# A two-layer decoder step on one core: the SSD group's small steps placed between the matmuls of the input projection, and the SSD half of the output projection taken first

## The chip, the cores and the metric

The kernel runs on one core of a Trainium2 chip. The metric is the device time of one execution in microseconds (us). The core has a matrix engine (PE, whose weight loads are listed apart as PEld), a vector engine (DVE), a scalar engine (ACT), GpSimd (POOL) and a queue engine (SP) that here only starts DMAs. Each engine works through its own list of instructions in order and waits on semaphores where another engine's result is needed.

## The reference, cut to what matters

320 tokens (256 of a prompt and 8 sequences of 8) of width 1024 go through two layers. Each layer is a mixer and a feed-forward part; layer 0 has a dense one, layer 1 a mixture of 8 experts.

```python
def parallel_mixer(hn, lb, w_in, conv_w, ..., w_out, s_hg, s_ssd, conv_buf):
    proj = jnp.einsum('bld,de->ble', hn, w_in)
    q, f, i, og, z, xbc, dt = jnp.split(proj, SPLIT_IDX, axis=-1)
    q = silu(q); log_f = logaddexp(log(lb), log1p(-lb) + log_sigmoid(f)); k_in = (1 - lb) * sigmoid(-f)
    o_hg, s_hg_new = hgrn2_chunked(q, k_in, i, log_f, s_hg)
    o_hg = rmsnorm(o_hg, hg_norm) * silu(og)
    conv = silu(conv_b + sum(conv_w[tap] * xpad[:, tap:tap + L]))   # 4 taps over xbc
    xs, bm, cm = jnp.split(conv, ...)
    dtf = softplus(dt + dt_bias); A = -exp(a_log)
    y, s_ssd_new = ssd_chunked(xs * dtf, dtf * A, bm, cm, s_ssd)
    y = rmsnorm((y + d_skip * xs) * silu(z), ssd_norm)
    return einsum('ble,ed->bld', concatenate([o_hg, y]), w_out), s_hg_new, s_ssd_new, conv_buf_new

for l in range(2):
    h = h + parallel_mixer(rmsnorm(h, norm_mix[l]), ...)
    h = h + (swiglu if l == 0 else moe_swiglu)(rmsnorm(h, norm_ffn[l]), ...)
return rmsnorm(h, norm_final), states
```

## The kernel before, in words

All matrix products with weights are done in three passes: a weight is split into a rounded high part (`spH`, made by ACT in `split_hi`) and the rest (`spL`, made by DVE in `split_lo`), and the activations likewise (`hnH`, `hnL`). PE runs high x high, high x low and low x high. Weights arrive in units of 1 MB in a ring of six places that SP fills; `split_hi` and `split_lo` turn a unit into one of two split buffers, and PE raises `used` when it has read one. A unit of the input projection is 32 matmuls with `spH` and 16 with `spL`, 320 columns each.

One layer's mixer has three stages on PE:

1. **The input projection**, 14 units: seven chunks of 512 output columns, each in two halves over the contraction, on PSUM banks 0 to 3 and 4 to 7 in turn. The order of the chunks is xs, B and C (together `xbc`), q, og, z, f, i. ACT evacuates each chunk. DVE runs the convolution over the first two chunks (`conv_in`), ACT its activation.
2. **The HGRN heads**: three token tiles (the 64 sample tokens first, then 128 and 128 prompt tokens; numbers 2, 0, 1) by four heads. For each head PE makes exponents (L1883, L1884), ACT their exponential (`M`), DVE the products (`Yq`, `Yk`), PE the scores (L1901 to L1908), DVE the mask (`SC`), PE the output (L1923). The states of the eight sample sequences lie in 16 slabs in the ring: eight of the HGRN group (k = 0), eight of the SSD group (k = 1). PE asks them (`ask`, L1960) in two steps for each group, ACT copies the answer (`said`), PE turns it (`turn_said`, L1968) and DVE adds it. Each HGRN slab is updated by a matmul (`sample_state`), an ACT scaling and a DVE add (`add_state`, L1375).
3. **The SSD group and the output projection.** After the last head PE goes through the SSD steps, for three tiles: transposes (`turn_tokens`, L1999, L2002), sums of the step sizes (`step_sums`, L2027), C times B (`groups`, L2051), decays from the start (`entry_sums`, L2039), the product inside a tile (`inside`, L2062), the prompt state (`prompt_ssd`, L2073), the carried state's part (L2154), and for the samples `ask(1, .)` and `sample_ssd` (L2089), whose slab is scaled by POOL and added to by DVE (`add_ssd`, L1352). Between them lie the squares for the HGRN norm (`group_squares`, L2100). Then come the four units of the output projection (`projected`, 7 us each): the HGRN half of the contraction on both column halves, the squares of the SSD group (L2212), and the SSD half.

The order within an engine is written out by hand in the source; there is no planner. SP loads the slabs after the output projection's weights, four slabs to a ring place, each place when the unit in it has been split.

Of the kernel before, what the change touches and what calls it, by code (L numbers as in the profile page):

```python
# [122 lines left out]
CHUNKS = [2560, 3072, 0, 1536, 2048, 512, 1024]  # L123
C_XS, C_BC, C_Q, C_OG, C_Z, C_F, C_I = range(7)
# [8 lines left out]
HG_BANKS = (2, 3, 2, 3)  # L133
# [7 lines left out]
ASK_AT = {(0, 1): 0, (0, 3): 1}  # L141
TOLD_AT = {(0, 2): 0, (1, 0): 1}
# [29 lines left out]
def build(nc, a, outs, table, at):  # L172
    y_prompt, y_sample, hg_p, ssm_p, conv_p, hg_s, ssm_s, conv_s = outs
    ctx = ExitStack()
    with ctx:
# [35 lines left out]
        def tabv(name, dt=F32):  # L211
            o, n = at[name]
            if o < nr:
# [21 lines left out]
        xdt = put("xdt", [P, NH * HD])  # L235
        xw = put("xw", [P, NH * HD])
        Bt = put("Bt", [P, G * P])
        SH = put("SH", [P, H * P])
        rstd = put("rstd", [P, TOK], offset=cursor[0] - 4 * H * P)
        SS = put("SS", [P, NH * HD])  # L240
        qGp = put("qGp", [P, H, P], offset=cursor[0] - 4 * NH * HD)
# [14 lines left out]
        wsm = put("wsm", [P, NH])  # L256
# [4 lines left out]
        cso = put("cso", [3 + NSQ * 3, CONV], offset=tok0 + 8 * CONV)  # L261
        Bm = put("Bm", [NS, NSQ, G * P], offset=tok0 + 17 * 1024)
# [8 lines left out]
        ea = put("ea", [P, NSQ * NH], offset=hn0 + 15 * 1024 + 512)  # L271
        am = put("am", [P, NSQ, NH], offset=hn0 + 15 * 1024 + 768)
        kd2 = put("kd2", [NS, H * P], offset=hn0 + 16 * 1024)
        vtk2 = put("vtk2", [NS, H * P], offset=hn0 + 18 * 1024)
        La = put("La", [P, NH, P], offset=ov + 4 * 1024)
        t1 = put("t1", [P, 4, P], offset=ov + 8 * 1024)
        CBm = put("CBm", [P, G, P], offset=ov + 10 * 1024)
        Mt = {2: M, 0: put("M2", [P, LV + 1, P], offset=tok0 + 4 * 1024), 1: M}
        Lat = {2: put("La2", [NS, NH, NS], offset=tok0), 0: La, 1: put("La1", [P, NH, P], offset=arena + 8 * H * TOK)}
        aext = {2: put("aex2", [NS, NH, HD], offset=tok0 + 2 * 1024)}  # L280
        xdtt = {2: xdt, 0: put("xdt1", [P, NH * HD], offset=tok0 + 2 * 1024), 1: xdt}
        xwt = {2: put("xw2", [NS, NH * HD], offset=hn0 + 16 * 1024), 0: xw,
               1: put("xw1", [P, NH * HD], offset=tok0)}
        Btt = {2: put("Bt2", [NS, G * P], offset=hn0 + 18 * 1024), 0: Bt, 1: Bt}
        EE2 = put("EE2", [P, 4, NS], offset=hn0 + 19 * 1024)
        aex = put("aex", [P, NH, HD], offset=sc0)
        aext[1] = aex
# [9 lines left out]
        sqs = put("sqs", [P, 4, TOK], offset=arena + 4 * H * TOK)  # L297
        rsh = put("rsh", [P, H, TOK], offset=arena + 8 * H * TOK)
# [90 lines left out]
        def slab(l, k):  # L389


            return ring[:, (PLAN["out", l] + 4 + k // 4) % RING, 512 * (k % 4):512 * (k % 4) + 512]
# [1303 lines left out]
        def _(pe):  # L1696
# [78 lines left out]
            for l in range(DEPTH):  # L1775
# [96 lines left out]
                def exponents(t, h):  # L1872
# [3 lines left out]
                    if j:  # L1876

                        pe.wait_ge(S("x_exp"), j)
# [561 lines left out]
```

## Time and profile before

| | us |
|---|---|
| median of 3 runs | 1767.23 (1765.89 to 1770.63) |
| the profiled execution | 1772.5, its span 1770.7 |
| mean granted clock of PE, share of full | 0.975 |
| PE busy | 1705.9 (96%) |
| DVE busy | 1291.2 (73%) |
| ACT busy | 1039.1 (59%) |
| POOL busy | 98.3 (6%) |

A row of the timeline gives start, duration, engine, line, operation, output and inputs, and in brackets how long the engine had been idle before it and what ended that. A row of the table by stretch gives, for each engine, the busy time and the number of instructions, then PE's granted clock (1.00 is 2.4 GHz, 0.50 is 1.2 GHz) and what the DMA engines moved. The profiled execution took 1.8 us more than its span. The stages after the mixers (dense feed-forward of layer 0, experts of layer 1) take from 272.7 to 525 us and from 775 us to the end.

### The profile page before, as it was taken

To read this page: it belongs to the slowest core of one execution; us is meant where nothing else is said; L and a number is where in the kernel's file an instruction comes from. 1 tells how busy PE (TensorE), PEld (TensorE's weight loads), DVE (VectorE), ACT (ScalarE), POOL (GpSimd) and SP (SyncE) were. 2 spreads that over 40 slices of the span, in tenths; PEclk is the share of its full clock that TensorE was granted. 3 is DMA by queue.
4 is the path that set the end of the run, shared out by engine and by line. 5 is a ranking of instruction groups with operands and counts; after the bars stand their busy time and mean duration, and the time that the engine had idled before them with its cause. 6 is when DMAs were issued, how large, how long until landed. Compare 5 with 4: busy or idle time off the path is not lost.

```text
span 1770.7 us, 23227 instructions
## 1 busy us (share of the span) xinstructions
PE 1705.9 (96%) x9594; PEld 1484.9 (84%) x9594; DVE 1291.2 (73%) x1119; ACT 1039.1 (59%) x942; POOL 98.3 (6%) x85
## 2 busy tenths in 40 slices
PE   8999889999999999789999999999999999999997
PEld 7988778999999978678888888888888888788876
DVE  6636655444357347649988888888888888888897
ACT  4444333333334344247777777777777777777776
POOL 2001120000000011202200000000000000000200
PEclk9997989999999989899999999999999999999999
DMA  9559153443553413249999999999999999899994
GB/s 298 167 162 269 49 171 115 155 148 99 147 169 121 165 39 84 60 179 331 391 394 396 397 371 384 374 382 395 362 379 379 368 397 389 317 394 370 373 394 175
DMA packets 272616, 474.07 MB, mean 268 GB/s; under 512 B 41578, under 2 KB 103266, under 8 KB 272504
## 3 DMA queue, kind: packets, MB, share of 16 engines
q1 hardware_dynamic: 266432, 452.37, 71.7%
q10 hardware_dynamic: 3368, 12.75, 2.2%
q0 software_dynamic: 2704, 7.39, 1.5%
q8 instruction: 78, 1.28, 0.3%
q14 instruction: 34, 0.28, 0.0%
HBM read 454.69 MB, written 29.84 MB: 274 GB/s over the span
## 4 chain that ended last, share of the span: by engine, by line
PE 88%; DVE 6%; issue 2%; ACT 2%; DMA 1%; ACTq 0%; DVEq 0%
PE ps L1712 16%; PE ps L1713 16%; PE ps L2355 11%; PE ps L1707 9%; PE ps L1708 9%; PE ps L2376 5%; PE ps L1806 4%; PE ps L2241 3%; PE ps L1923 2%; DVE spL L1592 1%; PE ps L2259 1%; PE ps L2394 1%; PE ps L1901 1%; PE ps L2203 1%; DMA ring<-in_w_exp_in_dram 1%
## 5 line engine op out<-in xcount | busy, mean ns | idle before, releaser
L1592 DVE TENSOR_TENSOR spL<-ring,spH 128x2048 fp32r<-128x2048 f32 x336 | 767.2, 2292 | 100.2 <-ACT spH L967 97.6
L967 ACT ACTIVATE spH<-ring 128x2048 fp32r<-128x2048 f32 x336 | 643.0, 1916 | 131.9 <-PE ps L2355 69.0
L1712 PE MATMUL ps<-spH,XH 128*128 128x512 f32 x896 | 354.6, 396 | 1.8 <-issue 1.8
L1713 PE MATMUL ps<-spH,XL 128*128 128x512 f32 x896 | 350.4, 391 | 0.0
L1050 DVE TENSOR_TENSOR spL<-ring,spH 128x2048 fp32r<-128x2048 f32 (+1 forms) x74 | 158.8, 2146 | 182.3 <-ACT spH L662 182.2
L1707 PE MATMUL ps<-hnH,spH 128*128 128x320 f32 x928 | 277.3, 313 | 4.0 <-DVE hnL L1065 2.2
L1708 PE MATMUL ps<-hnL,spH 128*128 128x320 f32 x928 | 275.6, 311 | 0.0
L662 ACT ACTIVATE spH<-ring 128x2048 fp32r<-128x2048 f32 (+1 forms) x74 | 133.5, 1804 | 187.7 <-PE ps L2241 73.6
L2355 PE MATMUL ps<-spL,XH 128*128 128x512 f32 x896 | 240.9, 391 | 1.2 <-DVE spL L1592 1.2
L2355 PEld LDWEIGHTS ps<-spL,XH 128*128 128x128 f32 x896 | 168.0, 188 | 38.3 <-DVE spL L1592 2.4
L1712 PEld LDWEIGHTS ps<-spH,XH 128*128 128x128 f32 x896 | 168.7, 188 | 36.1 <-issue 2.3
L1713 PEld LDWEIGHTS ps<-spH,XL 128*128 128x128 f32 x896 | 168.9, 189 | 34.0
L1707 PEld LDWEIGHTS ps<-hnH,spH 128*128 128x128 f32 x928 | 176.4, 190 | 7.4 <-issue 4.8
L1708 PEld LDWEIGHTS ps<-hnL,spH 128*128 128x128 f32 x928 | 176.4, 190 | 0.2
L1712 PE MATMUL ps<-spH,hTH 128*128 128x512 f32 x448 | 175.9, 393 | 0.0
L1713 PE MATMUL ps<-spH,hTL 128*128 128x512 f32 x448 | 175.0, 391 | 0.0
L2376 PE MATMUL ps<-spL,hTH 128*128 128x512 f32 x444 | 119.3, 390 | 0.0
L1712 PEld LDWEIGHTS ps<-spH,hTH 128*128 128x128 f32 x448 | 84.1, 188 | 17.8 <-issue 0.2
L1713 PEld LDWEIGHTS ps<-spH,hTL 128*128 128x128 f32 x448 | 84.2, 188 | 17.4
L2376 PEld LDWEIGHTS ps<-spL,hTH 128*128 128x128 f32 x444 | 83.3, 188 | 18.3 <-DVE spL L1592 0.5
L1806 PE MATMUL ps<-hnH,spL 128*128 128x320 f32 x448 | 70.3, 309 | 0.0
L991 ACT ACTIVATE hTH<-ps 128x512 fp32r<-128x512 f32 x56 | 33.6, 600 | 60.7 <-PE ps L2394 60.7
(365 smaller groups left out, 1796.2 us busy)
## 6 DMA issues: line engine op xcount, KB each, us to landing
ring<-in_w_exp_in_dram SPq DMA_DIRECT2D x224, 1024.0 KB, 8.8
ring<-in_w_exp_out_dram SPq DMA_DIRECT2D x112, 1024.0 KB, 8.7
ring<-in_w_in_dram SPq DMA_DIRECT2D x28, 1024.0 KB, 5.4
ring<-in_w_ffn_in_dram SPq DMA_DIRECT2D x22, 1024.0 KB, 5.1
token_rows<-token_rows ACTq DMA_DIRECT2D x1, 11776.0 KB, 40.5
ring<-in_w_ffn_out_dram SPq DMA_DIRECT2D x16, 704.0 KB, 4.6
ring<-in_w_out_dram SPq DMA_DIRECT2D x8, 1024.0 KB, 5.0
out_dram<-ring SPq DMA_DIRECT2D x32, 256.0 KB, 2.7
```

Source lines behind the costliest of these rows:

```text
L662: A(spH[:, u % 2, 0:n], raw(u, n), ACT.Copy).then_inc(S("hi_done"), 1)
L967: A(esplit(j)[0], src, ACT.Copy).then_inc(S("hi_done"), 1)
L1050: V.tensor_tensor(spL[:, u % 2, 0:n], raw(u, n), spH[:, u % 2, 0:n].bitcast(F32), ALU.subtract).then_inc(S("split_done"), 1)
L1592: V.tensor_tensor(lo, eslot(j)[0], hi.bitcast(F32), ALU.subtract).then_inc(S("split_done"), 1)
L1707: mm(out, w, x[0], start=start, stop=False)
L1708: return mm(out, w, x[1], start=False, stop=False)
L1712: mm(out, x[0], w, start=start, stop=False)
L1713: return mm(out, x[1], w, start=False, stop=False)
L1806: m = mm(ps[:, 4 * (c % 2) + i, 0:TOK], wL[:, k, i * P:(i + 1) * P], hnH[:, kk], start=False, stop=kk == KT - 1)
L2241: m = mm(ps[:, 4 * (j % 2) + 2 * half + i, 0:TOK], wL[:, k, i * P:(i + 1) * P], hnH[:, k], start=False, stop=k == KT - 1)
L2355: m = mm(ps[:, 2 * (c % 2) + i // 2, :], XH[:, kk, xs], wL[:, k], start=False, stop=kk == KT - 1)
L2376: m = mm(ps[:, 6 + q, :], tH[:, f], wL[:, k, 512 * q:512 * q + 512], start=False, stop=c == EC - 1 and f == 3)
```

## The change: what it does

Everything concerns the two mixers; the line numbers of the changed kernel differ.

- The chunks of the input projection come in the order xs, BC, f, i, q, z, og. The first two are as before. The other five are cut into ten units of 256 output columns by the whole contraction, `whole(0)` to `whole(9)`, on banks 0, 1 and 2, 3 in turn. Banks 4 to 7 are free for SSD steps.
- A unit has three slots for other PE work: after the high passes of its first 128 columns, after those of its second, and after its low passes. All SSD steps over tiles stand there, and so does the turning of the convolution state (`turn_conv`, before: right after the projection). Their DVE and ACT parts stand between the splits. ACT loads its function tables four times in a mixer where it did twice.
- In the HGRN heads the SSD slabs are asked first, at (2, 1) and (2, 3) (tile, head), the HGRN slabs at (0, 1) and (0, 3) as before. The product with z, the squares of the SSD group and its norm are done during the heads; one unit of the output projection is split at (2, 1), the other already in the input projection (before: at (0, 0) and (0, 1)). POOL scales all eight SSD slabs in one row after `ask(1)`. SP loads the SSD slabs first.
- The output projection takes the SSD half first. `sample_ssd(1)`, `group_squares(0)`, `sample_ssd(2)` and `group_squares(1)` stand between the column groups of its first unit, `sample_ssd(3)` behind it, `sample_ssd(0)` before the last head's output.

```diff
-CHUNKS = [2560, 3072, 0, 1536, 2048, 512, 1024]
-C_XS, C_BC, C_Q, C_OG, C_Z, C_F, C_I = range(7)
+CHUNKS = [2560, 3072, 512, 1024, 0, 2048, 1536]
+C_XS, C_BC, C_F, C_I, C_Q, C_Z, C_OG = range(7)
+NARROW = 10
...
-ASK_AT = {(0, 1): 0, (0, 3): 1}
-TOLD_AT = {(0, 2): 0, (1, 0): 1}
+ASKS = ((1, 0), (1, 1), (0, 0), (0, 1))
+ASK_AT = {(2, 1): 0, (2, 3): 1, (0, 1): 2, (0, 3): 3}
+TOLD_AT = {(2, 2): 0, (0, 0): 1, (0, 2): 2, (1, 0): 3}
...
+                def whole(k, slots):
+                    u, h = PLAN["in", l] + 4 + k, k % 2
+                    if k < 2:
+                        pe.wait_ge(S("proj_evac"), NARROW * l + 1)
+                    elif k < 4:
+                        pe.wait_ge(S("f_evac"), 2 * l + h + 1)
+                    else:
+                        pe.wait_ge(S("proj_evac"), NARROW * l + k - 1)
+                    pe.wait_ge(S("hi_done"), u + 1)
+                    wH, wL = unit(u, KT)
+                    for i in range(2):
+                        for kk in range(KT):
+                            high(ps[:, 2 * h + i, 0:TOK], wH[:, kk, i * P:(i + 1) * P], (hnH[:, kk], hnL[:, kk]),
+                                 start=kk == 0)
+                        for step in slots[i]:
+                            step()
+                    pe.wait_ge(S("split_done"), u + 1)
...
+                    for step in slots[2]:
+                        step()
...
+                whole(0, ((), (), ()))
+                whole(1, ((), (), ()))
+                whole(2, ((turn_conv,), (lambda: step_sums(2),), (small_sums, lambda: turn_inputs(2))))
+                whole(3, ((lambda: step_sums(0),), (lambda: turn_groups(2),), (lambda: step_sums(1),)))
+                whole(4, ((lambda: groups(2),), (lambda: entry_sums(2, 1, 4), lambda: entry_sums(1, 2, 5)),
+                          (lambda: inside(2),)))
+                whole(5, ((lambda: turn_inputs(0),), (lambda: turn_groups(0),), (lambda: groups(0),)))
+                whole(6, ((lambda: prompt_ssd(0, 5),), (lambda: inside(0),), (lambda: turn_inputs(1),)))
+                whole(7, ((lambda: turn_groups(1),), (lambda: groups(1),), (from_carried,)))
+                whole(8, ((lambda: inside(1),), (lambda: prompt_ssd(1, 4),), ()))
+                whole(9, ((), (), ()))
...
+                def forget_part(h):
+                    dve.wait_ge(S("used"), u + 4 + h + 1)
+                    V.tensor_scalar(lfT[:, 2 * h:2 * h + 2], ps[:, 2 * h:2 * h + 2, 0:TOK], -40.0, None, ALU.max
+                                    ).then_inc(S("f_evac"), 1)
...
                 def sample_ssd(j):
                     pe.wait_ge(S("mask_done"), 8 * l + 4 + j + 1)
-                    if j == 0:
-                        pe.wait_ge(S("xw_done"), LT(l, 2) + 1)
-                        pe.wait_ge(S("E_exp"), 2 * l + 1)
+                    if j == 1:
                         pe.wait_ge(S("sh_done"), 2 * l + 2)
-                    if j == 1:
-                        pe.wait_ge(S("ss_done"), 2 * l + 1)
                     pe.wait_ge(S("slab_done"), 16 * l + 8 + 2 * j)
...
                     scores(t, h)
                     if j + 1 == len(HEADS):
-                        turn_tokens(2)
+                        sample_ssd(0)
+                    if (t, h) in ((1, 1), (1, 2)):
+                        ssd_squares(h - 1)
...
-                step_sums(2)
-                groups(2)
-                entry_sums(2, 1, 4)
-                turn_tokens(0)
-                ask(1, 0)
...
-                projected(0)
-                pe.wait_ge(S("gsq_done"), 2 * l + 2)
...
+                projected(0, (lambda: sample_ssd(1), lambda: group_squares(0), lambda: sample_ssd(2),
+                              lambda: group_squares(1)))
+                sample_ssd(3)
                 projected(1)
```

In `projected`, `half, c = divmod(i, 2)` becomes `half, c = 1 - i // 2, i % 2`, and unit 1 waits for `slab_done` of all 16 slabs and for the second `grs_done`.

The first place is DVE in layer 0's input projection, right after the convolution; `cpk` is the packed convolution state, `spL` the low part of a unit, `lfT` the forget gates. Before:

```order
L1143 SCALAR_TENSOR_TENSOR cvt<-xbc,vec,cvt 128x344 x3
L1050 TENSOR_TENSOR spL<-ring,spH 128x2048
L1209 COPY cpk<-xbc 128x8x3
L1211 COPY cpk<-xbc 128x24 x8
L1050 TENSOR_TENSOR spL<-ring,spH 128x2048 x7
L1179 TENSOR_SCALAR lfT<-ps 128x1280
L1184 SCALAR_TENSOR_TENSOR kT<-kT,lbom,lfT 128x320 x4
```

And the same place in the changed kernel:

```order
L1164 SCALAR_TENSOR_TENSOR cvt<-xbc,vec,cvt 128x344 x3
L1071 TENSOR_TENSOR spL<-ring,spH 128x2048
L1200 COPY cpk<-xbc 128x8x3
L1202 COPY cpk<-xbc 128x24 x8
L1209 TENSOR_SCALAR lfT<-ps 128x640
L1294 SCALAR_TENSOR_TENSOR dtb<-dtb 128x24
L1296 SCALAR_TENSOR_TENSOR dtb<-dtb,bc 128x24
L1300 TENSOR_TENSOR am<-dtb,tab 64x64
L1219 TENSOR_TENSOR La_111<-tabR,dtb 64x512
L1209 TENSOR_SCALAR lfT<-ps 128x640
L1071 TENSOR_TENSOR spL<-ring,spH 128x2048
```

The evacuation of the forget gates, last of all before, now comes right behind the convolution, in two parts, and PE's third narrow unit waits for the first of them.

The second place is DVE between the last heads and the output projection; `ring` is a slab, `rss` and `rsh` the norms' factors of the SSD and the HGRN half, `hnL` the projection's input. Before, its last steps of the mixer:

```order
L1437 TENSOR_TENSOR cvT<-cvT,zT 128x1280
L1441 SCALAR_TENSOR_TENSOR oT<-oT,vec,rsh 128x320 x4
L1352 TENSOR_TENSOR ring<-ring,ps 128x512 x2
L1446 TENSOR_TENSOR hnL<-oT,hnH 128x1280
L1352 TENSOR_TENSOR ring<-ring,ps 128x512 x2
L1452 SCALAR_TENSOR_TENSOR cvT<-cvT,vec,rss 128x320 x4
L1456 TENSOR_TENSOR hnL<-cvT,hnH 128x1280
```

In the changed kernel, from the last HGRN slab (L1442) on; L1433 is the prompt's HGRN state:

```order
L1442 TENSOR_TENSOR ring<-ring,ps 128x512 x2
L1473 SCALAR_TENSOR_TENSOR cvT<-cvT,vec,rss 128x320 x4
L1419 TENSOR_TENSOR ring<-ring,ps 128x512 x2
L1480 TENSOR_TENSOR hnL<-cvT,hnH 128x1280
L1433 SCALAR_TENSOR_TENSOR SH<-SH,egp,ps 128x128 x4
L1419 TENSOR_TENSOR ring<-ring,ps 128x512 x2
L1485 TENSOR_TENSOR oT<-oT,ogT 128x1280
L1419 TENSOR_TENSOR ring<-ring,ps 128x512 x2
L1489 SCALAR_TENSOR_TENSOR oT<-oT,vec,rsh 128x320 x4
L1419 TENSOR_TENSOR ring<-ring,ps 128x512 x2
L1494 TENSOR_TENSOR hnL<-oT,hnH 128x1280
```

The SSD half's input, the last of all before, now comes behind the first of four `add_ssd`; the last `add_ssd` stands behind the HGRN norm.

The third place is PE in the heads of the sample tile, before (exponents, output, scores, exponents of the next head):

```order
L1883 MATMUL ps<-tabR,lfH 128x256
L1884 MATMUL ps<-tabR,lfL 128x256
L1923 MATMUL ps<-SC,vtk_109 128x64 x4
L1901 MATMUL ps<-Yq_103,Yk_104 64x64 x3
L1904 MATMUL ps<-qT,kT 64x64
L1883 MATMUL ps<-tabR,lfH 128x256
L1884 MATMUL ps<-tabR,lfL 128x256
L1923 MATMUL ps<-SC_105,vtk_109 128x64 x4
```

and in the changed kernel:

```order
L2058 MATMUL ps<-tabR,lfH 128x256
L2059 MATMUL ps<-tabR,lfL 128x256
L2135 MATMUL ps<-ring,cvT 32x128 x16
L2100 MATMUL ps<-SC,vtk_105 128x64 x4
L2076 MATMUL ps<-Yq_101,Yk_102 64x64 x3
L2079 MATMUL ps<-qT,kT 64x64
L2058 MATMUL ps<-tabR,lfH 128x256
L2059 MATMUL ps<-tabR,lfL 128x256
L2143 MATMUL ps<-tab,said 128x128 x4
L2100 MATMUL ps<-SC_103,vtk_105 128x64 x4
```

One `ask` (16 matmuls) and one `turn_said` (4 transposes) have come in; the same pair stands at heads (2, 3) and (0, 0).

## Rows read from the trace of the kernel before

**Rows 1.** The table by stretch: the stages of both mixers.

```profile
16.27:120.18 103.91, 103.40 (x707) 101.41 (x707) 60.13 (x88) 48.46 (x67) 0.00 (x0) 1.00 0.62 204
120.18:201.51 81.33, 74.76 (x560) 62.87 (x559) 47.36 (x78) 33.20 (x66) 8.29 (x8) 0.81 0.66 197
201.51:272.67 71.16, 61.91 (x480) 55.40 (x479) 40.66 (x66) 22.79 (x31) 15.80 (x13) 0.90 0.46 132
...
629.12:704.86 75.74, 69.15 (x560) 58.08 (x559) 47.40 (x78) 32.95 (x66) 8.35 (x8) 0.89 0.23 53
704.86:775.20 70.34, 61.09 (x472) 53.04 (x471) 40.56 (x66) 19.73 (x29) 16.25 (x15) 0.93 0.31 87
```

**Rows 2.** PE's timeline in layer 0: its waits, and one ask at either clock.

```profile
54.47 2.51 PE L1806 MATMUL ps<-hnH,spL 128*128 128x320 f32 x16
...
121.76 1.03 PE L1833 MATMUL ps<-tab,cpk 128*27 128x128 f32 x8 [1.42 <-ACT oT L767]
...
125.02 0.38 PE L1883 MATMUL ps<-tabR,lfH 64*128 64x256 f32 x1 [1.79 <-DVE lfL L1220]
...
154.19 1.08 PE L1960 MATMUL ps<-ring,qG 128*32 128x128 f32 x32
...
186.17 1.56 PE L1984 MATMUL ps<-vtk,kdm 32*128 32x128 f32 x16 [1.11 <-DVE ring L1375]
...
193.52 1.60 PE L1923 MATMUL ps<-SC,vtk 128*128 128x128 f32 x12 [1.05 <-DVE SC L1260]
...
216.44 1.09 PE L2062 MATMUL ps<-M,xdt 128*64 128x128 f32 x16 [2.69 <-DVE M L1300]
217.46 1.94 PE L1960 MATMUL ps<-ring,cvT 128*32 128x128 f32 x32
...
238.03 2.08 PE L2089 MATMUL ps<-xw,Bm 32*128 32x256 f32 x8 [5.60 <-DVE ring L1352]
```

**Rows 3.** Groups by line of PE's work from 198.3 to 240 us, shapes apart.

```profile
L2027 PE MATMUL ps<-tabR,La 128*128 128x128 f32 x32 | 4.0, 278 | 0.0
...
L2100 PE MATMUL ps<-sqh,tab 128*128 128x320 f32 x8 | 2.6, 446 | 0.0
...
L2005 PE MATMUL ps<-dtb,tabR 64*64 64x8 f32 x2 | 0.3, 210 | 0.0
```

**Rows 4.** DVE's timeline, layer 0.

```profile
64.95 0.75 DVE L1211 COPY cpk<-xbc 128x24 f32<-128x24 f32 x8
...
110.51 1.48 DVE L1179 TENSOR_SCALAR lfT<-ps 128x1280 f32<-128x1280 f32 x1
...
199.33 1.28 DVE L1375 TENSOR_TENSOR ring<-ring,ps 128x512 f32<-128x512 f32 x2
...
232.30 1.61 DVE L1437 TENSOR_TENSOR cvT<-cvT,zT 128x1280 f32<-128x1280 f32 x1
234.75 1.94 DVE L1441 SCALAR_TENSOR_TENSOR oT<-oT,vec,rsh 128x320 f32<-128x320 f32 x4 [0.84 <-ACT rsh L909]
```

**Rows 5.** ACT's timeline, layer 0: the HGRN norm.

```profile
232.47 0.94 ACT L905 ACTIVATE rsh<-ps,eps 128x320 f32<-128x320 f32 x2 [3.48 <-PE ps L2100]
233.45 1.27 ACT L909 ACTIVATE rsh<-rsh 128x1280 f32<-128x1280 f32 x1
```

**Rows 6.** The table by stretch, finer: around changes of the granted clock.

```profile
121.91:125.32 3.41, 1.62 (x14) 1.33 (x13) 0.68 (x1) 1.66 (x3) 1.02 (x2) 1.00 0.29 94
125.32:128.73 3.41, 3.41 (x16) 2.08 (x15) 1.08 (x5) 1.95 (x4) 0.00 (x0) 0.50 1.03 357
...
149.21:152.63 3.42, 3.42 (x20) 3.07 (x18) 0.00 (x0) 2.50 (x3) 0.00 (x0) 0.50 0.97 315
...
214.07:217.48 3.41, 1.04 (x19) 0.90 (x20) 3.38 (x7) 0.00 (x0) 1.07 (x1) 1.00 0.00 0
217.48:220.89 3.41, 3.41 (x38) 2.67 (x37) 3.38 (x7) 0.00 (x0) 0.00 (x0) 0.50 0.71 158
...
630.53:633.94 3.41, 1.69 (x13) 1.43 (x14) 0.68 (x1) 1.57 (x4) 1.02 (x2) 1.00 0.03 7
...
654.42:657.84 3.42, 3.42 (x20) 3.02 (x20) 0.21 (x1) 2.38 (x2) 0.00 (x0) 0.50 0.00 0
```

More of the change, by code:

```diff
@@ new lines, in _ @@
+                tables(LN_EXP)
+                act.wait_ge(S("gate_steps"), 4 * l + 2)
+                own(A(dtb[:, 2], dtb[:, 1], ACT.Exp, scale=-1.0))
+                A(dtb[:, 2], dtb[:, 2], ACT.Ln, bias=1.0).then_inc(S("dt_ln"), 1)
+                if l == 0:
+                    act.wait_ge(S("stage_in"), 16)
+                    A(tabR[:], stage[:], ACT.Copy).then_inc(S("setup_act"), 1)
+                split_hi(u + 7)
+                act.wait_ge(S("f_evac"), 2 * l + 2)
+                own(A(kT[:], lfT[:], ACT.Exp, scale=-1.0))
@@ new lines, in _ @@
+                act.wait_ge(S("gate_steps"), 4 * l + 4)
+                act.wait_ge(S("setup_dve"), 3)
+                for h in range(H):
+                    A(lfT[:, h], lfT[:, h], ACT.Ln, bias=lbom[:, l, 0, h:h + 1],
+                      scale=lbom[:, l, 1, h:h + 1]).then_inc(S("lf_done"), 1)
+                evacuated(2)
+                split_hi(u + 8)
+                act.wait_ge(S("w_mm"), l + 1)
+                for i, t in enumerate(ORDER):
+                    n = TILES[t][1]
+                    A(wsm[0:n, i], ps[0:n, 7, 256 + 8 * i:264 + 8 * i], ACT.Exp)
@@ new lines, in turn_conv, with sums @@
+                def turn_conv():
+                    pe.wait_ge(S("cpk_done"), 8 * (l + 1))
+                    pe.wait_ge(S("proj_evac"), NARROW * l + 2)
+                    for half in range(2):
+                        for k in range(4):
+                            m = nc.tensor.transpose(ps[0:27, 6 + half, k * P:(k + 1) * P], cpk[:, 4 * half + k, :], ident)
+                        m.then_inc(S("cso_tr"), 1)
+                def sums(t):
+                    return tabv("w")[:, LV * P:] if t < 2 else tabv("ws")[0:NS, LS * NS:]
@@ L1816, in _, with from_carried @@
+                def from_carried():
+                    pe.wait_ge(S("ss_done"), 2 * l + 1)
+                    for j in range(4):
+                        m = mm(ps[:, 5, j * P:(j + 1) * P], SS[:, j * P:(j + 1) * P], cvT[:, 6 + j // 2, P:2 * P],
+                               start=True, stop=True)
+                    m.then_inc(S("yx_mm"), 1)
+                for c in (C_XS, C_BC):
+                    if c == C_XS and l:
                         pe.wait_ge(S("rstd_done"), 2 * l + 1)
-                    if c == 1:
+                    if c == C_BC:
```

912 lines of the change are left out of this document (449 added, 463 removed).

## The prediction

> **What bounds the kernel now.** I read the table by stretch first, then PE's timeline. PE is busy 103.40 of the 103.91 us of layer 0's input projection: there PE itself is the bound, while DVE works 60.13 and ACT 48.46 us [rows 1]. In the heads and in the last stage PE has 6.6 and 9.3 us without work, and a granted clock of 0.81 and 0.90 [rows 1]. The waits of the last stage are few and long: 2.69 us for the masked decays `M`, 5.60 us for the second last slab addition behind the HGRN norm; in the heads 1.42 and 1.79 us at the entry and 1.11 and 1.05 us near the end [rows 2]. So an SSD step that is laid into the projection costs its own PE time there; only the waits and the half clock that follows them can be won.
>
> What they are worth: layer 0's waits after the projection are 15.9 us (81.33 + 71.16 less 74.76 + 61.91, with the rounding), and the clock of 0.90 over 71.16 us is some 10 to 14 us at half clock, of which 5.6 were idle; that is about 4 us. An ideal change would win about 20 us in a layer. The question is what it puts in their place.
>
> **The change part by part,** layer 0; the time of a unit of weights is 7.04 us (48 passes; the last 16 of them show as 2.51 us with their drain, 2.35 from start to start [rows 2]).
>
> a) *Input projection, work.* From 198.3 to 240 us the SSD steps that move there make 17 of the 26 groups, L2027's with 4.0 us the largest and L2005's with 0.3 the smallest [rows 3]; together 20.9 us, with `turn_conv` (1.03 us [rows 2]) 21.9. About 1 us of it is half clock. Every group's busy time ends later than the next one starts, by about 0.1 us, 22 to 25 times. I take 18.3 us. Bounds: 16.5 and 21.9.
>
> b) *Input projection, waits.* PE's third narrow unit waits for the evacuation of the first. DVE reaches it only behind the convolution and the packing, 65.7 us [rows 4], and it takes half of 1.48 us with its fixed part, 0.8. PE has finished two narrow units at 63.9 (49.8 and twice 7.04). The wait is 66.6 less 63.9, 2.7 us. I followed the remaining units by the rows' durations: DVE's split of a unit comes when ACT's is done, and ACT's when the unit two before has been read. Everything a slot needs is there, but for the mask of tile 0, which stands behind a split: 0.3 us. Sum 3.0. The other end is 9, 1 us at each of six units; its lower end is 2.4, as the first wait can't go.
>
> c) *Entry to the heads.* Before: 120.18 to 125.02, 4.8 us with `turn_conv` in it [rows 1, 2]. After: ACT evacuates half a chunk and loads a table, then the same chain of two copies; 3.6 us. Gain 1.2.
>
> d) *Asks among the sample tile's heads.* Twice an `ask` and a turning. The stretch runs at 1.2 GHz today: 27.3 us in layer 0 (eight rows from 125.32 to 152.63) and 17.1 in layer 1 (five rows, the last ends at 657.84) [rows 6]. There an ask costs 1.94 us instead of 1.08 [rows 2] and the turning about 1.0: 5.9 us. At full clock it is 3.4 and a wait of 1.1 behind the split at head (2, 1), which is then in DVE's way: 4.5. I take 5.9.
>
> e) *Later in the heads.* The product with z, 1.61 us [rows 4], stands ahead of the low gates that PE's next exponents wait for; about 0.6 us of it is covered: +1.0 (0 to 1.6). The SSD squares are four fp32 matmuls of 320 columns, like L2100's (2.6 us for four [rows 3]); they fall just ahead of the waits of 1.11 and 1.05 us [rows 2] and fill them: +0.2 (0 to 2.6).
>
> f) *The last head.* `sample_ssd(0)` needs the PSUM banks of the last HGRN slab, whose additions end at 200.6 [rows 4]. PE stands 2.2 us, works 1.1, then makes the last output, which before could start behind 1.3 us of transposes: +2.0.
>
> g) *From the last output to the end of the output projection,* before 71.16 us [rows 1]. After: the prompt state 1.0, a wait of 0.4 for `add_ssd(0)` and of 0.6 for `hnL`; four units 28.2; three `sample_ssd` 3.4 (2.08 in the row is at half clock [rows 2]); the two `group_squares` 2.6 less drains, 2.5. Then a new wait: unit 1 needs all slabs, and the last addition stands on DVE behind the norm. From the second squares ACT needs 0.94 and 1.27 [rows 5], DVE 1.94 and 1.3 [rows 4]: 5.6 with the hand-overs, of which 3.5 are covered by the low passes and `sample_ssd(3)`: 2.2. Sum 38.3. Gain 32.9 in layer 0, 32.0 in layer 1.
>
> Sum of a to g: 18.3 + 3.0 - 1.2 + 5.9 + 1.0 + 0.2 + 2.0 - 32.9 = -3.7 us in layer 0, -2.8 in layer 1.
>
> h) *POOL beside the heads.* Its eight scalings of slabs (part of 15.80 us busy [rows 1]) move to the first heads of the prompt tile. The trace has no such overlap there. Nothing if DVE never meets it, 3.6 if two of DVE's products each wait one scaling of up to 1.8. I take 1.0 a layer.
>
> i) *Half clock after the new waits.* A stretch with PE busy 1.04 of 3.41 us was followed by one at 0.50 [rows 6], which costs half of its 3.4 us where PE has work. There are three new candidates a layer (2.7 us in b; 2.2, 0.4 and 0.6 close together in f and g; 2.2 in g). Taken as an even chance each and rounded down: +1.7. Bounds 0 and 5.1.
>
> Total: -3.7 - 2.8 + 2.0 + 3.4 = -1.1; the half clock in the heads that followed the wait of 1.11 us in layer 0 may go with that wait, -1.7. That makes -2.8 us. The profiled execution took 1772.5 us, so 1769.7 in its terms; the runs' median is 1767.2, so 1764.5.
>
> *Hidden otherwise:* ACT's two extra table loads lie in the projection, where ACT works under half the time. The SSD slabs come when units 12 and 13 of the projection have been split, some 15 us before the first ask; SP's weight loads for the next stage start about 17 us before they are needed (24 before). The 11.8 MB of zeros that ACT starts in layer 0 still start at the entry to the heads.
>
> **A rule against the change.** Both layers enter the heads with PE busy 1.62 and 1.69 us of a stretch of 3.41, much of it transposes (L1833 and the gates'). In layer 0 the clock fell at once, in layer 1 it stayed at 1.00 two stretches longer [rows 6]. The Trainium skill says in "TensorE: Matmul & The Clock Gate", Part 4: PE-mode transpose, that transposes do not count as activity for the clock as matmuls do. By that rule both entries should have fallen; the trace agrees for one.
>
> **The rivals.**
> 1. *Both entries fall.* After the change only the gates' transposes stand in an entry of 3.6 us, so less work than in either row. Layer 1 then has the heads of layer 0: 81.33 less 75.74 is 5.6 us [rows 1], less 1.7 for a later stretch at half clock in layer 0: +3.9, so 1768.4. For it: less PE work; against it: the entry is shorter. The rule above would make this certain.
> 2. *The new waits and the half clock stay away* (faster). No half clock in i (-3.4), POOL meets nobody (-2.0), d at 4.5 (-2.8), e at nothing (-2.0): -10.2, so 1754.3; with half of these 1759. For it: PE's work in the slots fills the stretches; against it: each piece needs its own luck.
> 3. *DVE is late in the projection* (slower). Its chain is ACT's split, DVE's split, then an SSD step that the next slot reads; about 21 us of SSD work join the 60.13 [rows 1]. Should each of six units from the fourth to the ninth wait 1 us, that is +12 over both layers: 1776.5. It decides from about 0.7 us a unit. Against it: by the durations each step is ready 0.5 us or more before its slot, but for one.
> 4. *The steps don't land in the slots.* The order of PE shows them there; I give it nothing of weight.
>
> **How the numbers follow.** My forecast 0.35, rival 1 0.13, rival 2 0.31, rival 3 0.20, rival 4 0.01. The forecast's own range is 1760 to 1770. What a measurement can tell from no change is 0.3%, 5.3 us: faster is below 1761.9, slower above 1772.5. The forecast lies a tenth below 1761.9 and the rest between; rival 2 is faster, rival 3 mostly slower, and of rival 1 a quarter. Faster 0.35, same 0.42, slower 0.23. Likeliest 1764.5; the range takes in most of both sides: 1752 to 1777.
>
> **What would show it.** In the profile after: a wait of 2 to 3 us of PE for DVE's `lfT` in the projection of each layer, and that stage 21 us longer; waits of about 2 us ahead of `sample_ssd(0)` and of the output projection's second unit; 38 us from the last output to the projection's end; the heads 4 to 9 us longer. It is wrong if the projection grows by 27 or more (rival 3), if the clock stays at 1.00 through the entries, or if the last stage is not near 38.

## The result, and the profile after

The changed kernel took 1784.11 us (median of 5 runs, 1781.81 to 1787.9), the kernel before 1767.23 (5 runs, 1762.51 to 1774.47): a ratio of 1.0088, 95% interval 1.0066 to 1.011 (the ratio is taken over all runs of both; the quotient of the two medians is 1.0096). The forecast was 1764.5 us with a range of 1752 to 1777; the time lies above both. The profiled execution after has a span of 1780.0 us, against 1770.7.

The table by stretch of the kernel after (us, busy time of PE, PEld, DVE, ACT, POOL, granted clock, DMA share, GB/s) answers to [rows 1]: projection, heads and last stage of layer 0, then of layer 1; the last row leaves off the end of its stage.

```profile
15.41:142.90 127.49, 123.84 (x883) 119.13 (x884) 80.25 (x128) 58.32 (x91) 1.41 (x3) 0.99 0.56 170
142.90:241.32 98.42, 78.28 (x629) 64.96 (x627) 53.01 (x84) 35.66 (x67) 26.02 (x17) 0.80 0.53 170
241.32:279.71 38.39, 36.25 (x233) 33.61 (x232) 17.28 (x20) 13.10 (x12) 0.86 (x1) 0.97 0.71 205
532.28:658.22 125.94, 122.23 (x884) 117.65 (x885) 76.48 (x116) 54.76 (x86) 1.45 (x3) 1.00 0.39 113
658.22:742.00 83.78, 76.67 (x633) 63.87 (x631) 53.40 (x85) 36.24 (x68) 26.00 (x17) 0.86 0.20 56
742.00:778.70 36.70, 34.20 (x214) 31.42 (x214) 16.64 (x20) 9.43 (x9) 1.30 (x3) 0.95 0.41 116
```

What stands out is the second row: layer 0's heads take 98.42 us and layer 1's 83.78 for the same work; before they took 81.33 and 75.74 [rows 1]. PE has 20.1 us without work there. Its timeline in layer 0 says where, and answers to [rows 2]:

```profile
65.64 0.41 PE L1745 MATMUL ps<-hnH,spH 128*128 128x320 f32 x1 [2.47 <-DVE lfT L1209]
...
146.58 0.39 PE L2058 MATMUL ps<-tabR,lfH 64*128 64x256 f32 x1 [3.08 <-DVE lfL L1345]
...
189.51 0.87 PE L2135 MATMUL ps<-ring,qG 128*32 128x128 f32 x12 [13.65 <-DMA ring<-in_state_hgrn_dram]
...
236.43 1.17 PE L2171 MATMUL ps<-xw,kdm 32*128 32x256 f32 x5 [2.33 <-DVE ring L1442]
...
258.52 0.39 PE L1745 MATMUL ps<-hnH,spH 128*128 128x320 f32 x1 [2.14 <-issue]
```

Three of these five waits were in the forecast as waits, and the one of 3.08 us lies inside its entry of 3.6 us. The third was not: 13.65 us before `ask(2)`, the first ask of the HGRN slabs, in layer 0 alone. Before, the same ask stood there without a wait (154.19 in [rows 2]). The change loads the slabs in the other order, so the queues have to be read. SP's of the kernel before (start, issuing time, number of transfers):

```profile
103.58 9.06 SPq L457 DMA_DIRECT2D ring<-in_state_hgrn_dram  x8
155.98 12.68 SPq L457 DMA_DIRECT2D ring<-in_state_ssm_dram  x8
```

SP's of the kernel after:

```profile
122.76 11.04 SPq L462 DMA_DIRECT2D ring<-in_state_ssm_dram  x8
140.92 27.70 SPq L462 DMA_DIRECT2D ring<-in_state_hgrn_dram  x8
```

And the transfers of the kernel after from 140 to 190 us (KB each, median us from issue to landing):

```profile
token_rows<-token_rows ACTq DMA_DIRECT2D x1, 11776.0 KB, 45.8
ring<-in_state_hgrn_dram SPq DMA_DIRECT2D x8, 256.0 KB, 9.9
out_dram<-SS POOLq DMA_DIRECT2D x1, 256.0 KB, 6.1
```

The same zeros in the kernel before, which started at 122.8 us:

```profile
token_rows<-token_rows ACTq DMA_DIRECT2D x1, 11776.0 KB, 40.5
```

ACT starts the 11.8 MB of zeros at 143.11 us, and they land 45.8 us later, at 188.9. Before, the eight HGRN loads were issued by 112.6, ahead of the zeros, and the SSD slabs, which came under the zeros, were asked only behind 200 us. After, the HGRN slabs come in two fours, as places of the ring come free. The first four are issued from 140.9 to 142.4, ahead of the zeros, and land within 5.8 us. The other four are issued from 159.0 to 160.5, under the zeros:

```profile
DMA to landing us min/median/max: 14.0/23.3/28.9
```

They land one after another, 14.0, 21.4, 25.3 and 28.9 us after their issue, the last at 189.4. The first HGRN ask needs all eight and could have begun at 175.9: TensorE waits until 189.5. Layer 1 has no zeros and no such wait.

The rest of the ledger, by the two profiles: layer 0's mixer (projection to the end of its output projection) takes 7.9 us more, layer 1's 1.3 us less; without the 13.65 us they would be 5.8 and 1.3 us shorter. The start is 0.9 us shorter and the stretch behind layer 1's mixer 3.5 longer; about 4 us of that is idle time of TensorE near the start of the last expert pair, for which the trace names no engine:

```profile
1523.90 0.49 PE L1750 MATMUL ps<-spH,XH 128*128 128x512 f32 x1 [1.95 <-issue]
1529.23 0.59 PE L1751 MATMUL ps<-spH,XL 128*128 128x512 f32 x1 [3.91 <-issue]
```

The kernel before has one such wait, of 1.84 us. That makes 9 us in the profiles; the medians lie 17 apart, which is taken up below.

### The profile page after: what moved, and what is told of

The parts are those of the page before. It is cut to its first block, busy times and chain, and to the rows that moved or that the text cites. A ratio compares the mean times of both kernels' runs of the same rounds, so it can differ in the third digit from the quotient of the medians.

```text
span 1780.0 us, 23257 instructions
## 1 busy us (share of the span) xinstructions
PE 1705.6 (96%) x9594; PEld 1484.3 (83%) x9594; DVE 1295.3 (73%) x1121; ACT 1044.5 (59%) x956; POOL 106.6 (6%) x85
## 4 chain that ended last, share of the span: by engine, by line
PE 89%; DVE 5%; DMA 2%; issue 2%; ACT 1%; SPq 0%; DVEq 0%; ACTq 0%
PE ps L1750 17%; PE ps L1751 17%; PE ps L2419 11%; PE ps L1745 9%; PE ps L1746 8%; PE ps L2440 6%; PE ps L2305 3%; PE ps L1872 2%; PE ps L2100 2%; DMA ring<-in_state_hgrn_dram 2%; PE ps L2323 1%; PE ps L2458 1%; PE ps L2076 1%; PE ps L2271 1%; PE ps L1844 1%
## 5 line engine op out<-in xcount | busy, mean ns | idle before, releaser
L1750 PE MATMUL ps<-spH,hTH 128*128 128x512 f32 x448 | 175.9, 393 | 0.0
L1750 PEld LDWEIGHTS ps<-spH,hTH 128*128 128x128 f32 x448 | 84.1, 188 | 17.7
L1751 PEld LDWEIGHTS ps<-spH,hTL 128*128 128x128 f32 x448 | 84.2, 188 | 17.5
L2440 PEld LDWEIGHTS ps<-spL,hTH 128*128 128x128 f32 x444 | 83.4, 188 | 17.9
L642 POOL DMA_INDIRECT took<-token_rows,ixi x6 | 10.5, 1756 | 814.0 <-SPq L528 812.5
## 6 DMA issues: line engine op xcount, KB each, us to landing
token_rows<-token_rows ACTq DMA_DIRECT2D x1, 11776.0 KB, 45.8
```

What stands on the lines that cost most here:

```text
L1750: mm(out, x[0], w, start=start, stop=False)
L1751: return mm(out, x[1], w, start=False, stop=False)
L2440: m = mm(ps[:, 6 + q, :], tH[:, f], wL[:, k, 512 * q:512 * q + 512], start=False, stop=c == EC - 1 and f == 3)
```

## The experiments

Eleven edited kernels ran, and the changed kernel a second time, 5 to 12 executions each. Every ratio is to executions of the kernel before that were taken beside them; their medians were 1769.68 us for e1, e1p, c1 and e2, 1768.09 for e0, e3, e4 and e5, and 1769.57 for c2, e6, e7 and e8. Where kernels of different groups are compared below, a difference of medians therefore holds to a few us only, and the one by the ratios stands beside it.

**The zeros.** Three kernels: the changed one with the zeros later (e1), with 20 of their 23 blocks at the old place (e1p), and the kernel before with them later (c1).

```
-                if l == 0:
+                    if l == 0 and (t, h) == (0, 1):     # behind told(ASK_AT[t, h])
                     act.wait_ge(S("xs_zero"), 16)
                     act.dma_start(rows[CAP:, :]...)
```

> The changed kernel with one DMA moved: the 11.8 MB of zeros that ScalarE starts at the entry to layer 0's heads are started behind the third ask (head 1 of tile 0), when all sixteen slabs have landed. Theory A (the HGRN slabs, whose loads the change puts behind the SSD slabs, land only when the zeros have landed; that is the loss): the wait of 13.65 us before the third ask in layer 0 falls under 1 us, the asks behind it run at full clock, layer 0's stretch from the heads to the output projection falls from 98.4 to about 84 us (layer 1 has 83.8), and the time from 1784.1 to about 1769.5 (1766 to 1773). Rival B (the loads are slow by themselves, because SyncE issues eight of them in a row between 140.9 and 168.6 us): the wait stays over 8 us and the time over 1777. Rival C (the zeros take the same time from the slab stores and the weight loads that come next): the wait goes but over 5 us of it come back before the feed-forward layer, 1775 or more.

> The changed kernel with the zeros split in two transfers: 20 of the 23 blocks (10.2 MB) still start at the entry to the heads, 3 blocks behind the third ask. Theory A: the slabs land when the first transfer has landed; 45.8 us x 20/23 = 39.8 us, 6.0 us sooner, so the wait before the third ask falls from 13.65 to about 7.7 us (6 to 9.5) and the time by about 6 us, to 1778 (1775 to 1781). Rival B (slow loads by themselves): the wait stays within 1 us of 13.65. Rival D (it is the start of the big transfer that delays the loads, not its length): also unchanged.

> Control: the kernel before with the same move of the zeros (behind the first HGRN ask of tile 0). Its HGRN slabs land before the zeros start and its SSD slabs are asked some 20 us after the zeros have landed, so theory A expects no change: 1767.2, within 0.3% (1762 to 1772.5). If it gains 5 us or more, the zeros cost the kernel before something too, and the gain of the first run would say less about the change.

| kernel | median us | ratio [95%] | wait before `ask(2)` |
|---|---|---|---|
| after | 1784.11 | 1.0088 [1.0066, 1.011] | 13.65 |
| e1p, 20 of 23 blocks | 1779.55 | 1.0058 [1.004, 1.0076] | 7.89 |
| e1, zeros later | 1768.81 | 0.9989 [0.9971, 1.0007] | 0.49 |
| c1, before, zeros later | 1768.78 | 0.9994 [0.9974, 1.0014] | none |

The row of e1p and that of e1 at that ask:

```profile
185.99 1.94 PE L2138 MATMUL ps<-ring,qG 128*32 128x128 f32 x32 [7.89 <-DMA ring<-in_state_hgrn_dram]
```

```profile
177.21 1.08 PE L2135 MATMUL ps<-ring,qG 128*32 128x128 f32 x32 [0.49 <-DVE t L1410]
```

Theory A stands in what it says of the cause: the wait goes with the zeros, its length follows theirs (7.7 us were worked out beforehand for 20 blocks, 7.89 came), and the kernel before, whose order never puts a needed slab under them, gains nothing. In e1 the same eight loads land in 3.7 us (median, 5.0 at most), so rival B falls; the slab stores now take 8.7 us each under the zeros, but nothing came back from that (rival C). All three times lie in their ranges. The profile of e1p is of its second fastest execution (1770.41 us, with a median of 1779.55): that one escaped half clock in layer 1, as shown below. This one collision accounts for the loss: without it the time falls by 15.3 us (17.5 by the ratios), and e1 lies within 0.3% of the kernel before. In the profiles layer 0's heads take 82.0 us in e1 and 98.42 in the changed kernel, 16.4 more: the wait, and half clock for the ask and the matmuls behind it (1.94 us for the ask instead of 1.08).

The Trainium skill says in "DMA: Bandwidth & Descriptors", Queues, rings and completion order, that a DMA engine takes turns between queues packet by packet. This trace agrees, if what the profile counts as packets are the packets meant. The profile counts them for each queue (packets, MB, share of the DMA engines' time); in the kernel after, from 166 to 182 us, while zeros (q10) and loads (q1) run side by side:

```profile
q10 hardware_dynamic: 1166, 4.77, 85.5%
q1 hardware_dynamic: 1189, 0.59, 14.4%
```

That is one packet for one packet, but those of the zeros hold 4 KB each and those of the loads 0.5 KB (4.77 MB and 0.59 MB), so the loads get a ninth of the bytes. At that rate 1 MB in four loads takes some 28 us (an estimate: 2048 packets at 1189 in 16 us). So theory A's wording, that the slabs land when the zeros have landed, is too strong: three of the four land earlier, and the last, at 189.4, would by this estimate have come at about that time had the zeros gone on. A shorter transfer helps all the same (e1p), since the loads speed up when the zeros run out: from 182 to 188 us q1 moves 719 packets.

**The first wait in the projection.** In e2 the instruction `forget_part(0)` stands ahead of the last `conv_in`.

> The changed kernel with one VectorE instruction moved: the first copy of the forget gate's products out of the banks (0.82 us) is issued before the last of the eight convolutions instead of behind the eighth, a split and the packing of the convolution state. Theory: TensorE's wait of 2.47 us before the third 256-column unit goes in both layers (to under 0.2), nothing else moves by over 0.5 us, and the time falls by 4.9 us to 1779.2 (1777 to 1782). Rival: the split of the next unit, now 0.8 us later, is then the last thing in that unit or the convolution is, and under 2 us are gained (1782 or more).

Measured: 1775.01 us, 1.0028 [1.0013, 1.0044], below the range; the wait of 2.47 us is gone in both layers, and nothing took its place. That is 9 us under the changed kernel (10.6 by the ratios) and not 4.9; layer 1's heads were 2.6 us shorter (79.7 for 82.3) at more clock, so part of the surplus is of the kind treated next. A term of the forecast that I had called unavoidable (its "lower end is 2.4, as the first wait can't go") went by moving one instruction.

**The changed kernel again.** A surplus as in e2, and 17 us between medians where the profiles give 9, asked for a second timing.

> The changed kernel, not edited, timed again beside the kernel before: the recorded ratio of 1.0088 rests on five runs of each. In the two profiled executions the mixers account for +6.6 us, the start for -0.9 and the stretch behind the second mixer for +3.5 (9.3 us together), but the medians lie 17 us apart. If the difference of the profiles is the true one, the ratio comes out near 1.005; if the medians' is, near 1.009. I expect 1.008 (1.0065 to 1.009), 1783 us: in the changed kernel's profile both entries to the heads fall to half clock, and in the one run of the zeros experiments in which layer 1's entry did not, its heads took 76 instead of 82 us; the kernel before may escape that more often than its one profile shows.

Measured: 1783.67 us, 1.0083 [1.007, 1.0096]. The difference of the medians is real.

**The clock behind the entry.** Of the changed kernels, e1p had one layer whose heads took 76 us instead of 82. The stretch of 20 us that begins 4 us behind the entry's start, in layer 1 of e1 (the clock is the third number from the end):

```profile
650.20:670.20 20.00, 20.00 (x126) 15.41 (x128) 9.44 (x24) 6.25 (x10) 8.64 (x4) 0.52 0.20 56
```

The same of e1p:

```profile
658.40:678.40 20.00, 17.80 (x170) 13.65 (x169) 14.17 (x29) 8.62 (x13) 13.12 (x7) 0.91 0.19 55
```

At 0.52 (1.2 GHz for nearly all of it) PE is busy without a gap and makes 126 matmuls; at 0.91 (mostly 2.4 GHz) it makes 170 and has time left. Ahead of both stands the idle wait of 3.07 us at the entry, so the wait alone doesn't fix how long the clock stays down. In e5 it is filled, in c2 a part of the one of the kernel before.

```
                 turn_gates(ORDER[0])
+                hold(12, 5)          # e5, on e1: 12 unread matmuls of 512 columns
+                hold(6, 1)           # c2, on the kernel before
                 exponents(ORDER[0], 0)
```

> The kernel of e1 (zeros behind the third ask) with 12 matmuls of 128x512 whose result nobody reads, put on TensorE behind the gates' transposes at the entry to the heads of each layer, into a free bank: some 2.7 us of work in a wait of 3.07 us. Nothing else is moved and nothing can be saved but clock. Theory E (the wait at the entry is what drops the clock to 0.50 for some 20 us behind it): the clock stays at 1.00 from the entry on, the heads of each layer take 76 instead of 82 us as in the one execution in which layer 1's entry stayed up, and the time falls from 1768.8 to 1757 (1754 to 1761). Rival F (the clock falls for what the sample tile's heads themselves are, small matmuls with gaps): it falls all the same, and the time stays at 1768.8 (1766 to 1771).

> Control for e5: the kernel before with 6 matmuls of 128x512 (some 1.4 us) in its wait of 1.79 us at the entry to the heads, nothing else. If what the held entry gives back (17.7 us from e1 to e5, of which 5 lie behind the second mixer) is a property of both kernels, the kernel before gains too: its profile shows half clock from 4 to 32 us behind layer 0's entry and from 12 to 28 behind layer 1's. But it has two more idle pieces at the entry (1.42 us before the turning of the convolution's state) that stay. Theory E: 1760 (1756 to 1766). If it stays at 1768 (1766 to 1771), the held entry is worth something in the changed kernel alone, and the change made the entry worse for the clock.

e5: 1751.12 us, 0.9903 [0.989, 0.9916]; c2: 1764.39, 0.9976 [0.9958, 0.9995]. The same stretch in layer 0 and 1 of e5:

```profile
149.10:169.10 20.00, 18.30 (x174) 14.17 (x173) 14.47 (x29) 8.87 (x14) 12.41 (x7) 0.91 0.19 55
644.20:664.20 20.00, 18.37 (x175) 14.22 (x174) 14.42 (x29) 8.96 (x14) 12.65 (x7) 0.91 0.20 58
```

Matmuls that compute nothing save 17.7 us by the medians, 15 by the ratios, more than the range had: rival F falls, and theory E stands for the entry, where the clock is 1.00 for the first 12 us. It isn't 1.00 throughout: 16 us behind the entry a stretch of 4 us has 0.66 in layer 0, hence the 0.91. The heads take 77.7 us in both layers instead of 82.0 and 82.8, though the unread matmuls stand in them; that is 9.4 of the 17.9 us between the profiles of e1 and e5. Another 5.3 lie behind layer 1's mixer, where e5 lacks the second of the two unexplained waits, and 3.0 in the two last stages; why, no run here tells. The kernel before gains 5.2 us from the same trick (4.2 by the ratios), within the range of its forecast: its entry costs it something too, but less. So the changed kernel had both entries at half clock in the profiles of itself (0.53 and 0.53), of `e0_after_again` (0.53 and 0.51) and of e1 (0.54 and 0.52), while the kernel before had 0.50 and 0.63 (c2: 0.74 and 0.63). How much of the 8 us between profiles and medians this is stays open: that kernel's runs spread over 12 us (1762 to 1774), and its profiled run (1772.5) lies in their upper part.

**Real work in the same wait.** e4 puts `ask(0)` there and ACT's table load behind its copy of the gates; e6 adds the four masked copies of POOL behind the second ask.

```
                 turn_gates(ORDER[0])
+                ask(0)
-ASK_AT = {(2, 1): 0, (2, 3): 1, (0, 1): 2, (0, 3): 3}
+ASK_AT = {(2, 2): 1, (0, 1): 2, (0, 3): 3}
+                pool.wait_ge(S("ask_mm"), 4 * l + 2)      # e6, ahead of the masked copies
```

> The kernel of e1 with real work in the entry's wait: the first ask of the SSD slabs goes from head 1 of the sample tile to right behind the gates' transposes (1.08 us at full clock), the second from head 3 to head 2, and ScalarE copies the turned gates before it loads its table (1.28 us) and not after. The wait of 3.07 us should shrink to 3.07 - 1.28 - 1.08 = 0.7 us, and the stretch lose 1.28 + 1.94 (an ask at half clock) = 3.2 us a layer whatever the clock does: 1768.8 - 6.4 = 1762.4. If theory E holds and 0.7 us of idle time is little enough, 6 us a layer come on top: 1750. I expect 1751 (1748 to 1764).

> The kernel of e4 with GpSimd's four masked copies of the keys (2.1 us each) behind the second ask, out of the sample tile's heads. In e4 VectorE's short steps beside them took 1.20, 1.08, 0.95 and 1.21 us instead of 0.36, 0.17, 0.22 and 0.35, TensorE waited 3.91 us for the mask behind them, and the clock, which the ask at the entry had kept at 1.00 for 12 us, fell there. Theory G (VectorE and GpSimd hold each other up, and that wait drops the clock): the four steps return to their short times, the wait falls under 0.5 us, layer 0's and 1's heads fall from 82 to about 75 us and the time from 1768.9 to 1752 (1749 to 1758). Rival H (the clock falls at that place anyway, for the gaps between small matmuls): the wait goes but the clock still falls within 30 us of the entry, and the time only falls by the waits, some 6 us, to 1763. Rival I: the copies now lie beside tile 0's heads and cost VectorE there what they cost it before: 1765 or more.

e4: 1768.94 us, 0.9996 [0.9982, 1.0009]; e6: 1763.15, 0.9964 [0.995, 0.9978]. Both miss their ranges. In e4 the wait at the entry falls to 0.64 us, as worked out, and the clock stays at 1.00, but 12 us on the order turns against it. POOL of e4 there:

```profile
152.36 8.48 POOL L591 TENSOR_SCALAR kdm<-kd,tab 64x512 f32<-64x512 f32 x4 [6.45 <-DVE kd L1353]
```

DVE beside it, the products of the sample tile's last head:

```profile
156.23 1.20 DVE L1367 TENSOR_TENSOR Yq<-M,qT 128x192 f32<-128x192 f32 x1
157.35 1.08 DVE L1374 COPY egl<-M 128x8 f32<-128x8 f32 x1
158.47 0.95 DVE L1375 TENSOR_TENSOR qG<-M,qT 128x64 f32<-128x64 f32 x1
159.34 1.21 DVE L1377 TENSOR_TENSOR Yk<-M,kT 128x192 f32<-128x192 f32 x1
```

And PE behind them:

```profile
160.93 1.91 PE L2101 MATMUL ps<-SC,vtk 64*128 64x64 f32 x8 [3.91 <-DVE SC L1389]
```

The same four instructions two heads earlier, with POOL idle, took 0.36, 0.16, 0.23 and 0.35 us. PE then stands 3.91 us and the clock falls (1.91 us for what takes 1.10 at 2.4 GHz). In e6 the copies, released by the second ask at 152.6 us, still meet the same head: its product takes 1.20 us again, PE waits 2.50 and the clock falls (this profile is of the fastest of its twelve executions, 1758.04 us). Its time is the one rival H gave, but H wanted the wait gone first, and it isn't. Theory G's first half, that VectorE is held up beside GpSimd's copies, is shown; that the clock would stay up without the wait is borne out only by e7 below, which differs in other edits too and has no wait over 1.2 us left in these heads.

**The last head and the first unit.** e3, on e1: `output(last)` ahead of `sample_ssd(0)`, the prompt state step and `sample_ssd(1)` to `(3)` within unit 0, `mixed_f` ahead of the last mask, `add_ssd(3)` ahead of the norm's products.

```
-                projected(0, (lambda: sample_ssd(1), lambda: group_squares(0), lambda: sample_ssd(2), ...))
-                sample_ssd(3)
+                projected(0, (lambda: prompt_state(1), lambda: (sample_ssd(1), group_squares(0)),
+                              lambda: sample_ssd(2), lambda: group_squares(1)), lambda: sample_ssd(3))
```

> The kernel of e1 with the steps around the last head reordered: the output of the last head ahead of the first SSD state step, the prompt state step and all later ones between the thirds of the output projection's first unit, and on VectorE the SSD half's norm ahead of the last mask, the two slab additions that gate TensorE ahead of the norm's products. Theory (the waits predicted in terms f and g are what they seem, and the drain of the last head can be hidden): the waits of 2.33 us before the first SSD state step and of 2.14 us before the second unit go in both layers, and from the last output to the end of the projection it takes 38.4 - 3.5 = 35 us; with 1 us saved ahead of it about 4.7 us a layer: 1768.8 - 9.4 = 1759.4 (1757 to 1763). Rival (the chain through ScalarE's second norm sets the end of the first unit anyway): under 2 us a layer, 1765 or more.

Measured: 1756.26 us, 0.9922 [0.9908, 0.9936], just below the range; 12.5 us under e1, 11.9 by the ratios. The waits of 2.33 and 2.14 us are gone in both layers; what is left there is 0.59 us for `hnL`. From the entry to the start of the last low passes layer 0 takes 5.7 and layer 1 6.4 us less than in e1.

**Everything together.** e7 is e1, e2, e3 and e5 (with the table load behind the gates' copy and 7 matmuls); e8 has e6's real work instead.

> All of e1, e2, e3 and e5 together, and at the entry ScalarE's table load (1.28 us) behind its copy of the gates instead of ahead of it, so that the wait of 3.07 us falls to about 1.8 us, held with 7 of the unread matmuls. From e3's 1756.3: the forget copy 4.9, the table load 2.6, the clock behind the entry 12 us: 1736.8. I expect 1735 (1729 to 1742), 1.9% under the kernel before. If e5's whole 17.7 us come again it is 1731; if the clock falls in the new places, 1748.

> All of e1, e2, e3 and e6 together, with no unread matmuls: the ask of the SSD slabs fills the entry's wait, and GpSimd's copies stand behind the asks. If theory G holds, e6's gain over e1 comes on top of e3 and e2: 1756.3 - 4.9 - 17 = 1734 (1730 to 1744), about the same as the held version, with 3.2 us of real work saved a layer against a wait that stays a little open. If G fails and only the work is saved: 1756.3 - 4.9 - 6 = 1745.

e7: 1731.19 us, 0.9783 [0.9759, 0.9807], six runs between 1730.57 and 1731.89: 2.2% under the kernel before, as forecast. e8: 1749.43, 0.989 [0.9864, 0.9916], above its range and nearer to what it gave for theory G failing (1745). Projection, heads and last stage of e7's layer 0, against 127.49, 98.42 and 38.39 us of the changed kernel:

```profile
15.90:141.78 125.88, 123.36 (x888) 118.24 (x887) 82.45 (x132) 59.59 (x93) 1.42 (x3) 1.00 0.57 172
141.78:213.00 71.22, 66.33 (x626) 55.32 (x624) 51.19 (x82) 35.34 (x67) 26.21 (x17) 1.00 0.70 224
213.00:250.30 37.30, 36.62 (x244) 33.53 (x244) 18.50 (x22) 13.11 (x12) 0.86 (x1) 1.00 0.84 242
```

The granted clock is 1.00 through the mixers of both layers, and the six runs spread over 1.3 us, those of the other edited kernels over 3.7 to 12.4. That a clock which no longer falls there is the reason fits, but no run isolates it. In e8 the real work loses to POOL again. In layer 1 it is POOL's eight scalings.

```profile
646.42 8.04 POOL L601 TENSOR_TENSOR ring<-ring,ea 128x512 f32<-128x512 f32 x8
```

They meet one product of DVE:

```profile
648.63 6.78 DVE L1369 TENSOR_TENSOR Yq<-M,qT 128x896 f32<-128x896 f32 x1 [4.52 <-ACT M L852]
```

And PE waits for it:

```profile
656.80 1.97 PE L2103 MATMUL ps<-SC,vtk 64*128 64x64 f32 x8 [6.19 <-DVE SC L1391]
```

In layer 0 of the same run the same eight scalings (11.44 us) and the products beside them (1.22 to 1.93 us each) take turns; what decides between the two, no run here tells.

## Why the prediction was wrong

**The step that failed** is the paragraph "Hidden otherwise". It follows the SSD slabs, which the change moves to the front, and says of the zeros only that they "still start at the entry to the heads". Of the HGRN slabs, which the change moves to the back, it says nothing. The last four of them fall under those zeros and come 14 to 29 us after their issue, at a cost of 13.65 us of waiting and 15.3 us of the time. All of it could be read before: the zeros' 40.5 us at a DMA share near 1 (0.97 from 149.21 to 152.63 us [rows 6]), the ring slots that release each group of slabs, and where the first HGRN ask stands. Shown by e1, e1p and c1. With that one transfer out of the way the forecast would have held within the noise: e1's ratio is 0.9989 [0.9971, 1.0007], the forecast's is 1764.5/1767.2 = 0.9985.

Part of that is luck. In e1's profile layer 0's mixer is 6.3 us shorter than in the kernel before (the forecast's terms give 2.7), layer 1's is 0.6 us longer (0.1 shorter was forecast), and the stretch behind it is 2.6 us longer, for which the forecast had nothing. Errors of several us cancel.

**Projection (a, b).** The stage grew by 23.6 us in layer 0 (127.49 less 103.91), 21.3 were forecast. The waits are right: 2.47 and 0.68 us against 2.7 and 0.3. So the work was under-sized: 20.4 us against 18.3, inside its bounds; I had taken off too much for overlap between groups. (The 20.9 us in term a are the sum of 18 groups, not 17.) Rival 3 didn't happen.

**Entry (c).** 142.90 to 146.58 is 3.7 us, 3.6 were forecast. What I missed is in it: the two short pieces became one idle wait of 3.08 us.

**Heads (d to f, h).** In layer 1 they grew by 8.0 us; c to f and h come to 8.9. In layer 0 they grew by 3.4 beside the 13.65: its heads stood at half clock for 27.3 us before already, and for about 21 after. `ask` at half clock took 1.94 us as forecast, the waits of 1.11 and 1.05 us that the squares were to fill are down to 0.2 and 0.5, the wait before `sample_ssd(0)` was 2.33 against 2.2. POOL's cost (h) is small for TensorE in the changed kernel (some products of DVE take 1.6 to 1.9 us instead of 1.1, but TensorE's waits for the masks in the heads come to some 0.5 us a layer), but e4 and e8 show what was at stake: my end of 3.6 us for it was no upper bound, since one product alone took 6.78 instead of 1.09.

**Last stage (g).** 38.39 us against 38.3, with the new wait of 2.14 against 2.2. The best step of the forecast.

**Clock (i, rival 1).** I looked for the clock's fall behind the new waits. It fell behind the entry, in both layers of all profiles of the changed kernel: rival 1, to which I gave 0.13 and 3.9 us. The Trainium skill's rule on transposes that I quoted there ("TensorE: Matmul & The Clock Gate", Part 4) made this certain; the traces of the changed kernel agree, though e1p's layer 1 fell for 3 us only. No run tells the rule from the plain idle wait: e4 and e5, in which the clock stays up, put matmuls into the wait and so change both. e5 prices the matter higher, at 15 to 18 us in the changed kernel, and c2 at 4 to 5 in the kernel before.

What stays open: the unexplained waits at the last expert pair (1.8 to 5.9 us), and how the 8 us between the profiles' difference and the medians' divide.

## What to carry to other kernels

When a change swaps the order of two loads, follow the one that is moved back as carefully as the one moved forward, and hold each against every large transfer on any queue: count packets, not bytes. Loads in packets of 0.5 KB beside a transfer in packets of 4 KB got a ninth of the bytes here, and took 14 to 29 us instead of 3 to 5. A single idle wait of TensorE ahead of small matmuls, here of 3 us, can cost more than the wait; fill it, with unread matmuls if nothing else fits, and look whether the granted clock stays at 1.00. Real work in its place is only better if it doesn't push VectorE's short steps beside GpSimd's.

## What the runs showed of the hardware

- A DVE instruction can be held up by a row of POOL's for as long as the row lasts: 6.78 us for a product of 1.09 us, ending 1 us behind the eighth scaling (646.42 + 8.04). The Trainium skill, "SBUF — State Buffer", SBUF: two separate sides, says that a DVE instruction with two inputs in SBUF and a GpSimd one that reads SBUF take a shared port pair as an exclusive lock for the full instruction; this trace agrees, and here the waiting product didn't get its turn between back-to-back instructions of POOL. In layer 0 of the same run it did (1.22 us).
- Loads of 256 KB that took 3.7 us by themselves took up to 28.9 us beside a transfer of 11.8 MB on another queue. The two queues moved packet for packet (1166 and 1189 in 16 us), with 4 KB in the one's and 0.5 KB in the other's.
- Unread matmuls, 3.0 us of them in each layer, made a kernel 15 to 18 us faster (e1 to e5).
